# Queries of the differential heads turned by 32x32 squares and a DRAM exchange, in place of eight TensorE transposes

## The reference, cut to what matters

```python
def even_mixer(h, w_in, f_bias, qk_gains, ...):
    a_q, a_k, a_v, a_f, b_q, b_k, b_v = split_cols(h @ w_in, EVEN_SIZES)
    aq = rms_norm(a_q.reshape(bsz, seq, A_HEADS, HEAD_DIM), qk_gains[0])
    ...
    logf = jax.nn.log_sigmoid((a_f + f_bias).astype(jnp.float32))
    cum_logf = jnp.cumsum(logf, axis=1).transpose(0, 2, 1)
    a_out = forgetting_attention(aq, ak, av, cum_logf)
    bq = rms_norm(b_q.reshape(bsz, seq, B_HEADS, 2, HEAD_DIM), qk_gains[2])
    bk = rms_norm(b_k.reshape(bsz, seq, B_HEADS, 2, HEAD_DIM), qk_gains[3])
    bq, bk = apply_partial_rope(bq, cos, sin), apply_partial_rope(bk, cos, sin)
    b_out = differential_attention(bq, bk, bv, lam)
    ...

def forgetting_attention(q, k, v, cum_logf):
    s = q @ k^T * scale
    s = s + cum_logf[:, :, qs:qe, None] - cum_logf[:, :, None, :qe]
    ...
```

## Time and profile before

| what | before |
|---|---|
| median of the runs shown | 1864.44 us |
| profiled execution, its own time | 1865.1 us |
| span of the trace | 1862.7 us |
| PE busy | 1857.9 us (100%) |
| DVE busy | 1310.3 us (70%) |
| ACT busy | 1119.3 us (60%) |
| POOL busy | 369.0 us (20%) |
| TensorE clock granted | 1.0 in all of the span |

### The profile page before, as it was taken

The page is one execution under the profiler, slowest core; times in us unless marked ns, Lnnn a source line. Parts: engine busy times, 40 slices in busy tenths (PEclk is TensorE's granted clock), DMA queues, the critical chain, the costliest instruction groups (busy, mean ns, idle before and its releaser), DMA issues.

```text
span 1862.7 us, 25413 instructions
## 1 busy us (share of the span) xinstructions
PE 1857.9 (100%) x9293; PEld 1623.7 (87%) x9293; DVE 1310.3 (70%) x1949; ACT 1119.3 (60%) x1678; POOL 369.0 (20%) x606
## 2 busy tenths in 40 slices
PE   9999999999999999999999999999999999999999
PEld 8888988888889888888888889888888888899888
DVE  6776776667777776666577886776666578977664
ACT  6776655557766655555468785654555467765553
POOL 2101233111001431122103001531122111102320
PEclk9999999999999999999999999999999999999999
DMA  9767789878578997798765567997798788758984
GB/s 316 236 186 229 222 258 299 260 233 253 166 221 242 292 287 232 219 272 255 238 180 191 174 191 204 281 274 237 225 255 252 227 265 242 216 157 232 255 258 138
DMA packets 289803, 436.43 MB, mean 234 GB/s; under 512 B 25548, under 2 KB 170416, under 8 KB 289424
## 3 DMA queue, kind: packets, MB, share of 16 engines
q1 hardware_dynamic: 260384, 352.41, 61.9%
q0 software_dynamic: 28832, 82.07, 16.3%
q10 hardware_dynamic: 464, 0.34, 0.1%
HBM read 396.43 MB, written 38.29 MB: 233 GB/s over the span
## 4 chain that ended last, share of the span: by engine, by line
PE 99%; DMA 0%; DVE 0%; SPq 0%; ACT 0%; issue 0%; ACTq 0%
PE M L1081 31%; PE M L1083 31%; PE M L1082 31%; PE AUX L1124 1%; PE AUX L1138 0%; PE AUX L1252 0%; DMA RAW<-in_w_in 0%; PE AUX L1244 0%; PE AUX L1242 0%; PE AUX L1279 0%; PE AUX L1167 0%; PE AUX L1295 0%; PE AUX L1323 0%; PE AUX L1296 0%; PE AUX L1297 0%; PE AUX L1324 0%
## 5 line engine op out<-in xcount | busy, mean ns | idle before, releaser
L1647 DVE TENSOR_TENSOR WL<-RAW,WH 128x1024 fp32r<-128x1024 f32 (+1 forms) x669 | 810.8, 1217 | 383.5 <-ACT WH L1358 380.9
L1358 ACT ACTIVATE WH<-RAW 128x1024 fp32r<-128x1024 f32 (+1 forms) x670 | 705.0, 1055 | 518.8 <-PE M L1083 469.7
L1081 PE MATMUL M<-WH,Bh 128*128 128x512 f32 (+1 forms) x1820 | 691.3, 380 | 0.6 <-ACT TMP L1401 0.3
L1082 PE MATMUL M<-WL,Bh 128*128 128x512 f32 (+1 forms) x1820 | 683.1, 375 | 0.0
L1083 PE MATMUL M<-WH,Bl 128*128 128x512 f32 (+1 forms) x1820 | 683.1, 375 | 0.0
L1081 PEld LDWEIGHTS M<-WH,Bh 128*128 128x128 f32 x1820 | 344.2, 189 | 50.6 <-issue 4.2
L1083 PEld LDWEIGHTS M<-WH,Bl 128*128 128x128 f32 x1820 | 344.2, 189 | 47.1
L1082 PEld LDWEIGHTS M<-WL,Bh 128*128 128x128 f32 x1820 | 344.4, 189 | 44.7
L1396 ACT ACTIVATE AS<-M,KEEP 128x256 f32<-128x256 f32 x132 | 55.3, 470 | 80.3 <-PE M L1083 78.7
L1081 PE MATMUL M<-WH,MTh 128*128 128x512 f32 x128 | 51.0, 398 | 0.0
L1082 PE MATMUL M<-WL,MTh 128*128 128x512 f32 x128 | 48.5, 379 | 0.0
(11 more groups left out here) (534 smaller groups left out, 2886.9 us busy)
## 6 DMA issues: line engine op xcount, KB each, us to landing
RAW<-in_ffn_w_in SPq DMA_DIRECT2D x352, 256.0 KB, 4.2
RAW<-in_w_in SPq DMA_DIRECT2D x103, 512.0 KB, 4.8
RAW<-in_w_gate_up SPq DMA_DIRECT2D x176, 256.0 KB, 4.4
RAW<-in_ffn_w_out SPq DMA_DIRECT2D x88, 512.0 KB, 4.6
RAW<-in_w_down SPq DMA_DIRECT2D x44, 512.0 KB, 4.9
RAW<-in_x_w_kv SPq DMA_DIRECT2D x32, 512.0 KB, 4.6
RAW<-in_even_w_in SPq DMA_DIRECT2D x24, 512.0 KB, 4.5
RAW<-in_odd_w_in SPq DMA_DIRECT2D x24, 512.0 KB, 5.4
```

Of the source, the lines that this page charges most:

```text
L1081: e.matmul(out, s.hi, wh, start=s.at0, stop=False)
L1082: e.matmul(out, s.hi, wl, start=False, stop=False)
L1358: e.activation(hi, raw, ACT.Copy).then_inc(k.w_hi, 1)
L1647: e.tensor_tensor(lo, raw, hi.bitcast(F32), ALU.subtract).then_inc(k.w_lo, 1)
```

## The change

The queries of the differential heads take the exchange instead of the transposes. The two buffers that the exchange needs are `QA` (squares) and `KA` (what comes back), which stand empty until `aq` and `ak`. The assertion that an exchange has no rotation goes, and `bq` gets other due times: 7.8 for the squares (before: 9.8 for both groups of transposes) and 21.2 for ACT's copies into `QB`.

```diff
 PLACES = {
-    "bq": (3.2, 3.5, 9.8, 9.8), "bk": (3.2, 3.8, 10.4, 9.2), ...
+    "bq": (3.2, 3.5, 7.8, 21.2), "bk": (3.2, 3.8, 10.4, 9.2), ...
@@ head_qk
         if room is not None:
-            assert f.rope is None
             self.heads_out(x_at, y_at, "hn", f, s.xs, *room, lab, form, dst, gain)
             return s
@@ even_mixer
         c = self.chunk("bq", B, 0, KD, lab)
-        self.head_qk(c, nm, 8, "bq", ("plain", cols(QB), 0.125, 0))
+        room = [[Rows(x[:, :, :].rearrange("p k c -> p (k c)"))] for x in (QA, KA)]
+        self.head_qk(c, nm, 8, "bq", ("plain", cols(QB), 0.125, 0), room)
```

## The result

The changed kernel takes 1871.15 us in the median of 8 runs, the kernel before 1864.78 in the same session: a ratio of 1.0032, 95% interval 1.0023 to 1.0041. It is slower by 6.4 us; the forecast was +0.9, with a range up to 1867.6. The profiled execution took 1870.48, its span is 1868.4 (before: 1865.1 and 1862.7).

A forecast was written before the change was run, and what follows sets the result against it. PE, 99% of the chain of waits, was taken to bound the kernel. Transposes removed, -0.76, plus PE's wait behind the late forget gate, +1.7, gave +0.9 us: 1864.44 to 1865.3, range 1863.6 to 1867.6.

The forecast's parts named there:

- The transposes removed: Even mixer near 965: without eight transposes L1228 starts at 965.23 instead of 965.99, so PE gains 0.76 us.
- L1228 waiting for L1923: PE near 965: L1228 still needs L1923, which ends unmoved at 965.18, so it starts at about 965.23, not 965.12.
- the weight subtractions: DVE behind 965: transposes by squares push two weight subtractions back by 1.30 us; cost taken as 0, at most 1.3.
- the copies into `QB`: ACT: two copies from about 982.0 end near 983.2; PE wants them at 983.9, so 0.7 us spare, cost 0.
- When the exchange is through: POOL: DMA out at 968.1, first back pass 5.5 us later at 973.6, POOL free at 975.8, last landing 979.4.
- The rule that I weighed: Exchange's way out: about 2.0 us plus bytes over 436 GB/s, so 3.2 us; the forecast went by longer profile rows.
- What is queued behind it: POOL: forget gate's row out (L2155) goes 5.4 us later, at 975.8; 13.2 us to `nctown` kept, which ends at 1005.1.
- Who waits for it: DVE's `nctma` (L2055) stands still 2.0 us for `nctown`; PE loses 1.7 us at the first transposes of `ak`.
- 0.3 for slack: PE at the first transposes of `ak`: 0.2 to 0.4 us of DVE's lateness is free, taken as 0.3.
- rival B: Forget gate's rows much later, exchange and copies both slow: PE loses over 4.5 us, net over +3.7; chance 0.07.
- The claim that no gap absorbs DVE's stop: DVE from 1000.43 to the end of `ak`'s `hn`: busy 15.32 of 15.67 us, so next to no gap.

## Why the prediction was wrong

*The transposes removed*: -0.76 forecast, -0.74 measured. *L1228 waiting for L1923*, *the weight subtractions*, *the copies into `QB`* (at 982.33, with no wait for the landing): as forecast, within 0.4 us.

*When the exchange is through*: the squares end at 967.9 (967.6 forecast), the way out goes at 968.45 (968.1), the way back starts at 974.97 (973.6): it took 6.52 where I chose 5.5, inside my bounds of 4.19 and 6.9. The row out was 1.3 late by both. The rule that I weighed (the Trainium skill, "DMA: Bandwidth & Descriptors", section "Anatomy of one DMA — SWDGE (gpsimd) path"), with its estimate of 3.2, is not borne out by this trace's 6.52.

*What is queued behind it* is **the step that failed**: "I leave the 13.2 as they are, with 1 us either way." From the row out to the first `nctown` it took 994.24 - 977.14 = 17.1, so 3.9 more. I had seen that weight loads come on at about 979 and gave them 1 us; on the copies they cost 4.5 (13.36 against 8.89), since the late copies land beside the loads that go out from 979.7 on, not ahead of them; the small row in front landed 0.6 sooner. My own sum said so: the copies of 974.72, moved by 5.4, start at 980.1, behind the 979 that I name. `nctown` itself took 14.4, not 16.1. It ended at 1008.6, not 1005.1: 1.3 + 3.9 - 1.7 = 3.5 later.

*Who waits for it*: the mechanism was right, from POOL's L2165 over L2055 and L1824 to PE's transposes. DVE came to L2055 at 1004.27 (1003.1 forecast) and stood 4.36 us, not 2.0. Of this PE lost 2.60 + 1.70 = 4.3; I subtracted 0.3 for slack, and 0.06 would have been right. The place was not as forecast: I reckoned with `ak`, where the margin is least, but the transposes of `aq` have only 4.36 - 2.60 = 1.76 to spare, and a stop of 4.36 shows there first. That 1.70 of it would be lost at the low clock I had not foreseen, but the run that kept PE busy shows it to be inside the 4.3, not on top: there the rest of DVE's stop comes at `ak`.

Two terms were missing from the forecast: 0.56 at the first value product, where late weights stop ACT with PE's copy behind it, and 0.59 + 0.61 near 1610, of the buffers rotated by one. The sum for the profiled execution: 0.40 - 0.74 + 0.56 + 4.30 + 1.20 = 5.72, its lag at the end; the median moved by 6.4.

So rival B came about, past the point I named (`nctown` after 1007.9), and I gave it 0.07 because I held that a slow exchange and slow copies would have to fall together. The copies needed no slow exchange: the one that started at 977.9 took 11.29 and those from 980.6 on took 13.22 and more, and the forecast's own 980.1 lies between them. The claim that no gap absorbs DVE's stop held.

## What to carry to other kernels

A DMA that is moved later must be priced at what the queues carry at its new time; its old duration belongs to its old place: here copies issued 6.2 us later landed 10.6 us later. Look for what stands behind the waiting instruction on each in-order engine: moving one mask addition behind other work, or one small DMA ahead, took off some 4.5 us without speeding anything up. Eight transposes were worth 0.7 us, and the losses around the exchange could be taken out, but no version here is measurably faster than the kernel before.

## What the runs showed of the hardware

- After PE had stood still for 2.37 us its granted clock fell to 0.50, under 1 us after it had resumed, and came back by 1016.85: 1.70 us lost. Kept busy through that time it stayed at 1.00.
- Two copies of 1.5 MB together landed in 8.35 to 9.64 us or in 13.22 to 13.84, by whether they started ahead of a burst of weight loads or behind it; 11.29 in one trace lies between, and is not explained. With the weight loads held, late ones took 9.30.
- From the way out of an exchange through DRAM to its way back it took 0.9 to 1.9 us more or less by which of several equal buffers it used: near 968, 4.83 and 4.88 in the fifth, 6.26 to 6.72 in the first (two and seven traces); near 1598, 5.04 to 5.32 in the last of four, 6.19 to 6.51 in the first (six and eight). The first buffer is not slow everywhere: near 1613 it took 4.2. Why it is slow where it is, no run here tells.
